# Second mixer and four norms of a two-block transformer kernel: one-column sums of squares, a factor spread by products with ones, and a new order of the second mixer's work

## The reference

```python
def rms_norm(x, gain=None):
    y = x * lax.rsqrt(jnp.mean(x * x, axis=-1, keepdims=True) + EPS)
    return y if gain is None else y * gain

def modulate(x, shift, scale):
    return rms_norm(x) * (1.0 + scale) + shift

# layer 0: mixer with latent attention and pooling, then ffn;  layer 1: gqa_mixer, then ffn
xl = xl + ml[:, 2] * mixer(modulate(xc, ..), modulate(xl, ml[:, 0], ml[:, 1]))
xl = xl + ml[:, 5] * conv_ffn(modulate(xl, ml[:, 3], ml[:, 4]), ..)
# (in layer 0 the context xc goes the same way)

def gqa_mixer(hc, hl, w_in, g_q, g_k, w_out, cos, sin):   # layer 1: 8 query heads, 2 key heads, width 128
    q = apply_rope(rms_norm(heads(hl @ w_in[:, :1024]), g_q), cos, sin)
    k = rms_norm(heads(h @ w_in[:, 1024:1280]), g_k)       # of context and of x; rotated for x alone
    v = heads(h @ w_in[:, 1280:])
    return softmax(q @ k.T / sqrt(128)) @ v @ w_out        # each query over 768 keys
```

## Time and profile before

| | before |
|---|---|
| median of three runs | 2988.4 us |
| profiled execution, its own time | 2990.08 us |
| its span in the profile | 2988.4 us |
| mean granted clock of TensorE, share of full speed | 0.956 |
| TensorE busy | 2739.5 us (92%) |
| VectorE busy | 1605.2 us (54%) |
| ScalarE busy | 1021.9 us (34%) |
| GpSimd busy | 81.9 us (3%) |

### The profile page before, as it was taken

One profiled execution on the slowest core, in us unless ns is written; L12 is line 12 of the kernel. 1 busy time (PEld: TensorE's weight loads), 2 busy tenths in 40 slices (PEclk: granted clock), 3 DMA queues, 4 the chain that ended last, 5 costly groups with the idle time before them and its releaser, 6 DMA issues. The chain is left out here.

```text
span 2988.4 us, 35774 instructions
## 1 busy us (share of the span) xinstructions
PE 2739.5 (92%) x14414; PEld 2206.9 (74%) x14414; DVE 1605.2 (54%) x2338; ACT 1021.9 (34%) x1595; POOL 81.9 (3%) x108
## 2 busy tenths in 40 slices
PE   5979988999999968887999998899988999999997
PEld 3758876888888857775788875688865777777775
DVE  5568745433433466765544444255545665565566
ACT  2135533222222233543323324422233433343343
POOL 0100000000000000000000000000000000000000
PEclk8979998999999979998999999999998999999998
DMA  5430012232332211001222223222221222222221
GB/s 209 142 113 29 20 45 99 100 119 99 113 116 103 89 39 43 29 34 38 88 96 92 92 85 113 77 85 85 88 91 49 87 77 74 80 87 80 85 74 43
DMA packets 67241, 246.94 MB, mean 83 GB/s; under 512 B 7504, under 2 KB 7888, under 8 KB 66384
## 3 DMA queue, kind: packets, MB, share of 16 engines
q1 hardware_dynamic: 51280, 185.10, 17.6%
q0 software_dynamic: 14768, 55.51, 5.9%
q10 hardware_dynamic: 1040, 4.12, 0.4%
HBM read 242.45 MB, written 2.24 MB: 82 GB/s over the span
## 5 line engine op out<-in xcount | busy, mean ns | idle before, releaser
L1966 DVE TENSOR_TENSOR WL<-RAW,WH 128x1024 fp32r<-128x1024 f32 x331 | 405.3, 1225 | 686.7 <-ACT WH L1417 685.1
L689 PE MATMUL PS<-HM,WH 128*128 128x512 f32 x1752 | 707.1, 404 | 23.3 <-DVE HM L1973 10.9
L690 PE MATMUL PS<-HM,WH 128*128 128x512 f32 x1752 | 699.5, 399 | 0.0
L691 PE MATMUL PS<-HM,WL 128*128 128x512 f32 x1752 | 698.7, 399 | 0.0
L1417 ACT ACTIVATE WH<-RAW 128x1024 fp32r<-128x1024 f32 x331 | 349.7, 1057 | 821.1 <-PE PS L691 810.4
L689 PEld LDWEIGHTS PS<-HM,WH 128*128 128x128 f32 x1752 | 333.5, 190 | 99.7 <-issue 34.2
L691 PEld LDWEIGHTS PS<-HM,WL 128*128 128x128 f32 x1752 | 333.1, 190 | 80.4
L690 PEld LDWEIGHTS PS<-HM,WH 128*128 128x128 f32 x1752 | 333.7, 190 | 56.0
L689 PE MATMUL PS<-GM,WH 128*128 128x512 f32 x468 | 189.1, 404 | 15.4 <-DVE X_M L2473 11.7
L691 PE MATMUL PS<-GM,WL 128*128 128x512 f32 x468 | 188.4, 403 | 0.0
L690 PE MATMUL PS<-GM,WH 128*128 128x512 f32 x468 | 188.4, 403 | 0.0
(11 more groups left out here) (366 smaller groups left out, 4621.0 us busy)
## 6 DMA issues: line engine op xcount, KB each, us to landing
RAW<-in_tiles SPq DMA_DIRECT2D x333, 512.0 KB, 3.2
MRAW<-in_mods POOLq DMA_DIRECT2D x80, 512.0 KB, 5.0
TB<-bias_rows POOLq DMA_DIRECT2D x16, 576.0 KB, 6.3
FIRST<-in_mods SPq DMA_DIRECT2D x8, 1024.0 KB, 23.8
X_M<-in_x ACTq DMA_DIRECT2D x1, 2048.0 KB, 16.7
VN_GB<-in_gm_rows POOLq DMA_DIRECT2D x2, 1024.0 KB, 6.0
out_x<-X_M SPq DMA_DIRECT2D x8, 256.0 KB, 2.0
X_C<-in_ctx ACTq DMA_DIRECT2D x1, 1024.0 KB, 19.8
```

Source lines behind the costliest of these rows:

```text
L689: pe.matmul(out_, wh, xh, start=first, stop=False, skip_group_check=True)
L690: pe.matmul(out_, wh, xl, start=False, stop=False, skip_group_check=True)
L691: return pe.matmul(out_, wl, xh, start=False, stop=last, skip_group_check=True)
L1966: dve.tensor_tensor(WL[:, s.mod(2), :], RAW[:, s.mod(2), :], f32(WH[:, s.mod(2), :]), ALU.subtract).then_inc(tile_split[s.mod(2)], 1)
```

## The change

**Norms (mix0, ffn0, mix1, ffn1).** VectorE leaves out the last of the seven adds: `SUMSQ` holds seven squares. TensorE's `norm_sum` multiplies each 128x128 block of `SUMSQ`, and of the last `SQ`, as stationary operand by one column of ones: 6 blocks (4 in ffn1) x 2, one column of PSUM per block, tokens on partitions. ScalarE's root and VectorE's inverse are of 128x6. VectorE multiplies the identity by that column, block by block (`RB`, 128x768, diagonal blocks; called the diagonal below), and TensorE's `norm_spread` multiplies ones by `RB`, so that every partition has the factor in PSUM, where `scaled` reads it. `add_square(m)` stands behind the next chunk's `add_gated`. In ffn0 `mod_rows(21)` stands between `norm_sum` and `norm_spread`.

**Key norms.** The same for each key head (`key_sums`, `key_scale`, `key_scales`); ScalarE copies the raw keys to SBUF, and `key_norm` scales that copy.

**Second mixer's start.** The value tiles and the first two query tiles change places in the list of tiles; queries 0 and 1 are made ahead of the values.

**Loop.** In pairs 0 to 2 each rotation is cut in two (`query_parts`, `query_turned`) and spread over units n = 2 to 7; before, both were whole at n = 2 and 4. In pair 3 the update of `X_M` (`part_added`) stands ahead of `pt_low`.

```diff
+            def norm_sum(name, ctx_too):
+                ...
+                    for b in range(low_block, BLOCKS):
+                        mm = pe.matmul(norm_sums(name)[:, b:b + 1], squares[:, b * P:(b + 1) * P], ONES[:, 0:1], start=first and b == low_block,
+                                       stop=last, skip_group_check=True)
+                ...
+                pe.wait_ge(sq_summed, (KC - 2) * (at + 1))
+                block_sums(SUMSQ, True, False)
+                pe.wait_ge(sum_sq, KC * (at + 1))
+                block_sums(SQ[:, (KC - 1) % 2, :], False, True).then_inc(sum_used, 1)
+
+            def norm_spread(name, ctx_too):
+                pe.wait_ge(diag_ready, SPREAD[name])
+                if ctx_too:
+                    pe.matmul(rb_ctx(name), ONES[:, :], RB[:, 0:TC], start=True, stop=True, skip_group_check=True)
+                pe.matmul(rb_main(name), ONES[:, :], RB[:, TC:TA], start=True, stop=True, skip_group_check=True).then_inc(rb_spread, 1)
...
-                stats(name, KC, ctx_too)
+                norm_sum(name, ctx_too)
                 if mods:
                     mod_rows(21)
+                norm_spread(name, ctx_too)
...
+                    if n == 1 and k == 2:
+                        key_sums(0)
+                    elif n == 1 and k == 6:
+                        key_scales(0)
...
-            key_sums(0)
-            tile_ready(s + 2)
-            tile_ready(s + 3)
-            v_step(0)
-            key_sums(1)
-            v_step(1)
-            v_step(2)
...
-            project(0)
+            project(0, 0, 9)
+            key_sums(1)
+            project(0, 9, 18)
+            key_scales(1)
+            project(0, 18, 24)
             project(1)
+            tile_ready(s + 4)
+            tile_ready(s + 5)
+            v_step(0)
             query_sums(0)
+            v_step(1)
+            v_step(2)
             scores(0)
...
                 dve.wait_ge(rms_ready, n + 1)
-                dve.reciprocal(RB[:, lo:TA], RB[:, lo:TA]).then_inc(rb_ready, 1)
+                root, blocks = NORM_ROOT[:, lo // P:BLOCKS], BLOCKS - lo // P
+                dve.reciprocal(root, root).then_inc(rb_ready, 1)
                 dve.wait_ge(rb_ready, n + 1)
+                dve.tensor_tensor(RB[:, lo:TA].rearrange("p (b n) -> p b n", b=blocks), IDENT[:, :].unsqueeze(1).to_broadcast([P, blocks, P]),
+                                  root.unsqueeze(2).to_broadcast([P, blocks, P]), ALU.mult).then_inc(diag_ready, 1)
...
-            def out_part(m):
+            def part_added(m):
...
+                if pair == 3 and n:
+                    part_added(n - 1)
                 pt_low(w)
                 if w >= 2 and w % 2 == 0:
                     out_low((w - 1) // 2)
                 if pair < 3:
                     if n == 2:
-                        split(At(TILES["gqa_q"] + j + 2))
-                        query_rope(j)
+                        query_parts(j)
                     elif n == 3:
+                        query_turned(j)
+                    elif n == 4:
+                        split(At(TILES["gqa_q"] + j + 2))
                         query_low(j)
-                    elif n == 4:
-                        split(At(TILES["gqa_q"] + j + 3))
-                        query_rope(j + 1)
                     elif n == 5:
                         scale_of_queries(pair + 1)
+                        query_parts(j + 1)
+                    elif n == 6:
+                        query_turned(j + 1)
+                    elif n == 7:
+                        split(At(TILES["gqa_q"] + j + 3))
                         query_low(j + 1)
...
-                    out_part(n - 1)
+                    next_out_tile(n - 1)
```

More of the change, by code:

```diff
@@ L429, in build, with query_tile @@
                 LOAD_ORDER[gmlp_out(g)[0].start + m] = TILES["gmlp"] + 12 * g + 8 + m
+        for n in range(2):
+            LOAD_ORDER[TILES["gqa_kv"] + 2 + n] = TILES["gqa_q"] + n
+            LOAD_ORDER[TILES["gqa_q"] + n] = TILES["gqa_kv"] + 2 + n
+        def query_tile(j):
+            return At(TILES["gqa_kv"] + 2 + j if j < 2 else TILES["gqa_q"] + j)
         assert sorted(LOAD_ORDER) == list(range(N_TILES))
@@ L535, in stat_ctx, with norm_sums, rb_main, rb_ctx @@
             return PS[:, 4 if name == "mix0" else 5, 0:TC]
+        BLOCKS, CTX_BLOCKS = TA // P, TC // P
+        def norm_sums(name):
+            at = TC if name == "mix0" else 0
+            return PS[:, 5 if name == "mix0" else 7, at:at + BLOCKS]
+        SPREAD = {name: n + 1 for n, name in enumerate(("mix0", "ffn0", "mix1", "key0", "key1", "ffn1"))}
+        NORM_ROOT = CONST[:, 11:11 + BLOCKS]
+        def rb_main(name):
+            return PS[:, 2, :] if name in SUMMED else RB[:, TC:TA]
+        def rb_ctx(name):
+            return PS[:, 5, 0:TC] if name in SUMMED else RB[:, 0:TC]
         MOD_SUMS = PS[:, 6, 0:2 * P]
@@ L801, in _ @@
                 first_rows(pair)
+                if pair == 7:
+                    norm_spread("mix0", True)
                 first_turn(pair - 1)
@@ L804, in _ @@
                     pe.wait_ge(bias_ready, 1)
[L805 removed]
+                    norm_sum("mix0", True)
             first_turn(7)
@@ L1044, in key_sums, with key_scales @@
                     pe.wait_ge(head_rms, n)
[L1045 to L1046 removed]
+                for b in range(BLOCKS):
+                    mm = pe.matmul(key_cols(n)[:, b:b + 1], SQ[:, n, b * P:(b + 1) * P], ONES[:, 0:1], start=True, stop=True, skip_group_check=True)
+                mm.then_inc(head_sum, 1)
+            def key_scales(n):
+                pe.wait_ge(diag_ready, SPREAD[f"key{n}"])
+                pe.matmul(PS[:, 5, 0:TC], ONES[:, :], RB[:, 0:TC], start=True, stop=True, skip_group_check=True)
+                pe.matmul(PS[:, 4, :], ONES[:, :], RB[:, TC:TA], start=True, stop=True, skip_group_check=True).then_inc(rb_spread, 1)
             s = At(TILES["gqa_kv"])
@@ L1457, in root @@
                     act.wait_ge(sum_used, SUMMED.index(name) + 1)
-                else:
-                    act.wait_ge(sq_used, c0 + chunks)
+                    blocks = slice(0 if ctx_too else CTX_BLOCKS, BLOCKS)
+                    act.activation(NORM_ROOT[:, blocks], norm_sums(name)[:, blocks], ACT.Sqrt, bias=CONST[:, eps:eps + 1], scale=1.0 / features
+                                   ).then_inc(rms_ready, 1)
+                    return
+                act.wait_ge(sq_used, c0 + chunks)
                 if SPLITS.get(name, 0):
@@ L1747, in next_out_tile, with key_high @@
                     kept_chunks(m + 2)
-            v_taken(0)
-            v_taken(1)
-            for n in range(2):
+            def key_high(n):
                 act.wait_ge(rope_done, 10 + n)
@@ L1754, in _ @@
                 copy(KG[0][:, n, TC:TA], RG[0][:, :]).then_inc(key_hi, 1)
-                if n == 0:
-                    v_taken(2)
-                    for j in range(2):
-                        split(At(TILES["gqa_q"] + j))
+            key_high(0)
             query_taken(0)
+            key_high(1)
+            query_taken(1)
+            v_taken(0)
             query_high(0)
-            query_taken(1)
             root_of_queries(0)
             query_high(1)
+            v_taken(1)
+            v_taken(2)
+            for j in range(2):
+                split(At(TILES["gqa_q"] + 2 + j))
             exps(0)
@@ L2374, in down @@
                         add_gated(u + m, layer, 5, At(m), ctx_too)
+                        if before is not None and m:
+                            add_square(before, m - 1, 0 if ctx_too else TC)
                         if ahead and (m + 1) % per_tile == 0:
                             split(s + m // per_tile + 2)
-                        if before is not None:
-                            add_square(before, m, 0 if ctx_too else TC)
                 for f in range(FC):
@@ L2409, in _ @@
             s = At(TILES["gqa_kv"])
-            for n in range(2):
-                split(s + 2 + n)
             dve.wait_ge(norm_ready, SPLITS["ffn1"])
@@ L2478, in out_part @@
                     kept_chunks(m + 2)
+            split(s + 2)
+            key_scale(0)
             key_norm(0)
-            v_read(0)
+            split(s + 3)
+            key_rope(0)
+            key_scale(1)
             key_norm(1)
-            v_read(1)
-            key_rope(0)
-            v_read(2)
-            for j in range(2):
-                split(At(TILES["gqa_q"] + j))
+            split(s + 4)
             key_rope(1)
@@ L2494, in _ @@
             dve.tensor_scalar(ROPE_TG[:, 1, :], ROPE_TG[:, 1, :], LN[:, 2, 16:17], None, ALU.mult).then_inc(rope_gain, 1)
-            query_rope(0)
+            split(s + 5)
+            query_parts(0)
+            query_turned(0)
             query_low(0)
-            split(At(TILES["gqa_q"] + 2))
-            query_rope(1)
+            query_parts(1)
+            query_turned(1)
+            v_read(0)
             scale_of_queries(0)
             query_low(1)
```

(5 more changed lines are left out.)

108 lines of the change are left out of this document (68 added, 40 removed).

## The result

Four runs of the changed kernel: median 2950.03 us (2948.74 to 2953.86), beside 2990.18 for four of the kernel before; ratio 0.9868, 95% interval 0.9851 to 0.9885. A second set of four (e10) gave 2951.8 and 0.9874 (0.9858 to 0.9891). The prediction was 2959.3, within 2943 to 2975: the direction and this range held. The profiled execution has a span of 2952.2 us, 36.2 less than before's.

What follows compares the result with a forecast made beforehand. TensorE, busy for 2739.5 of 2988.4 us, was taken as the bound. Seven terms summed to -29.1 us, giving 2959.3 against the median of 2988.4; own range 2951 to 2966, widened by rivals to 2943 to 2975.

Steps and rivals of the forecast that it cites:

- seven terms: Forecast by stretch: mix1 -5.4, mix0 -1.1, ffn0 -1.5, ffn1 -6.0, start +6.5, loop -5.8, pair 3 -15.8 us.
- One sign of being right: In the changed profile, the loop's longest wait for `PTA` would be near 1 us.
- term of the output with ffn1: Output's updates and ffn1's norm: later adds and a smaller inverse give -6.0 us (-6.6 to -4.2).
- mix0: Norm of mix0: scaled chunks start 1.1 us earlier, -1.1 (-3.6 to +1).
- mix1: Norm of mix1: compact inverse and later adds against 24 one-column instructions, -5.4 us (-7.6 to -2).
- ffn0: Norm of ffn0: spread waits behind the second module rows' transfer, chunks begin 1.5 us sooner, -1.5 (-3 to 0).
- Start: Second mixer's start: old waits go, two new stalls from VectorE's order come, +6.5 us (-5 to +8).
- Rival 1: Second mixer's start pays, no stalls: -5 us there and not +6.5, 2948 in all; chance 0.14.
- Loop: Pairs 0 to 2: wait for `PTA` falls from 4.8 to about 1.1, -5.8 us (-14.5 to 0).
- Pair 3: Pair 3: TensorE's waits for `X_M` and the low clock behind them go, -15.8 us (-8 if `pt_low` takes half).
- Rivals 2, 3 and 4: 2: loop and pair 3 return less, 2973, chance 0.16; 3: clock stays low, slower, 0.03; 4: norms return nothing, 2971, 0.07.

Runs made afterwards that it cites:

- e10: The changed kernel run again, unedited: median 2951.8 us, ratio 0.9874 to the kernel before.
- e3: The kernel before with only the four norms changed: median 2969.15 us, ratio 0.9931.
- e5: The changed kernel with the second key's inverse and diagonal put ahead of the first key's low parts on VectorE: median 2946.38 us, ratio 0.9866.
- e6: The changed kernel with the second mixer's start reordered at both places where TensorE waited: median 2942.81 us, ratio 0.985.
- e2: The kernel before with only the loop's query rotations cut in two and spread over units 2 to 7: median 2979.89 us, ratio 0.9968.
- e4: The kernel before with only the second mixer's start changed: median 2991.9 us, ratio 1.001.
- e1: The kernel before with only pair 3's residual update put ahead of the transposed rows' low part: median 2973.63 us, ratio 0.9939.
- e7: The changed kernel with six products of each pair's second query moved from unit 2 to unit 3 in the loop: median 2951.2 us, ratio 0.9869.
- e11: The kernel before, unedited, once more for one profile: pair 3 took 72.4 us, where the first profile had 73.9.
- e8: The changed kernel with the edits of e6 and e7, and ffn0's spread ahead of the second module rows: median 2941.66 us, ratio 0.9843.

## Why the prediction was right, and what it mis-sized

**The places.** All seven terms have the right sign, and the waits named came where they were put: 4.1 and 3.7 us in the start (4.3 and 3.9 forecast), none for `X_M` over 0.3 in pair 3. One sign of being right failed: the loop's longest wait for `PTA` is 3.1 us and not near 1. The errors don't cancel: five terms were too small a gain or too large a loss by 1 to 3.5 us each, and only pair 3's was too large a gain, by 0.6 to 2.1.

**Norms.** The term of the output with ffn1 held (6.0, measured 6.0). mix0 can be read once the thirteen profiles are sorted by how long TensorE is busy before its sums: 21.2 us in five, 26.6 in eight, and both norms occur in both groups. Where it is 26.6, the first product behind the norm comes at 63.5 to 64.2 us in the five profiles with the old norm and at 61.1 to 61.7 in the three with the new one. Where it is 21.2, it comes at 59.2 in the one profile with the old norm, and with the new one at 56.2, 56.4, 56.8 and, in e3, at 59.2. So mix0 gave about 2.5 us where 1.1 were forecast, with one profile that shows none of it; some 1.5 lies ahead of the sums and so outside the table's stretch. mix1 gave 6.7 and not 5.4: the sums came 0.7 us earlier than I had them, and their first half ran faster, 12 instructions in 1.74 us and only the other 12 in 2.70. I had priced all 24 at 0.21 us, 5.1 in all; they end 4.3 after their start. The low-clock price itself is nearly right (0.225 an instruction for my 0.21; the bounds were 0.115 and 0.23). The Trainium skill's figure for a load of 128 columns that names no clock ("TensorE: Matmul & The Clock Gate", "LDWEIGHTS (loading the stationary operand)") does not hold at the lower clock: 12 loads would take 1.3 us by it, an estimate from its 107 ns, and the second twelve of mix1's norm took 2.68 at PEclk 0.50. ffn0 gave 2.5 and not 1.5: I had held the second module rows to the transfer's landing, 6.9 us behind its issue (468.5 to 475.4); in the changed kernel it landed after 5.9 (465.5 to 471.5), and the spread came that microsecond sooner.

**Start.** +6.5 was +5.1, and 0.8 less again from `scores(0)` to the first transposes. The waits and the clock behind them were nearly right (1.5 us on the spread, where I had 1.7, and 1.3 on the first value step, where I had 1.5); the order was the cause (e5, e6). The terms of that step add up to 6.1 and its chain of times to 6.4, not 6.5. Measured against its terms, idle time rose by 1.4 us (1.8 forecast) and TensorE's busy time by 3.7 (4.3 forecast). Rival 1, the start without its stalls, is what e6 is: 3.1 us less than before, where I had given 5.

**Loop.** This is the step that failed in size: 5.8 forecast, 9.3 measured, whole by itself (e2). The step counted waits, and waits fell by 6.2 us, near the forecast: idle time was 21.6 before (131.07 less 109.47 busy) and is 15.4 after (121.80 less 106.40). What it left out stood in the earlier trace rows: transposes that took 1.51 us behind the wait of 4.8, at the lower clock, for 0.84 now. TensorE's busy time fell by 3.1 us with the same instructions, and that is clock. I had added that price in the start and in pair 3 and not here. In the old loop slower products do cost time, because behind the long wait TensorE sets the pace: units 6 and 7 of pair 0 take 10.5 us there with 0.3 of idle time, and the old loop of e4, busy for 0.8 us less with the same idle time, is 0.8 shorter. In the new loop they no longer do: these units take 10.9 us with 2.4 of idle time, and the whole loop of e6, at clock 1.00, is as long as the changed kernel's at 0.98.

```profile
1164.84:1286.62 121.78, 105.16 (x669) 90.36 (x668) 91.23 (x171) 69.95 (x115) 0.00 (x0) 1.00 0.07 22
```

**Pair 3.** 15.8 forecast; 15.2 less than the first profile of before and 13.7 less than the second, 16.6 and 15.0 in e1. The old order takes 71.1 to 73.9 us in six profiles, with 12.6 us of idle time in each: up to 2.8 us of it is what the clock happened to be. I had taken the low clock of the longest of them (5.82 and 7.07 us) as a fixed price. And the new loop takes 1.3 us back in the first unit of pair 3, which is 9.65 for 8.31 in e1. That is VectorE's order and not the clock: in e7, with the clock at 1.00 all through pair 3, the unit takes 9.66 too, with a wait of 1.31 for `GM`.

**Sum.** The stretches with an edit give -36.4, where the terms gave -29.1: loop 3.5, start 2.1, mix1 1.3, ffn0 1.0, pair 3 -0.6. The second pair of profiles (e11 and e10) gives -34.6. What the timed runs show beyond that, 2 to 6 us, is in part mix0's earlier sums (some 1.5) and otherwise within what the stretches without an edit differ by from one execution to the next. Rivals 2, 3 and 4 did not come: the mean clock went from 0.956 to 0.967 and 0.969.

## What to carry to other kernels

When a wait on TensorE goes, count the slower products behind it too, in every stretch alike, but only where TensorE sets the pace: where it waits again soon after, the lower clock uses up that wait and costs nothing (e7 and e8, pair 0). So don't read idle time turned into busy time as a loss before a second profile, at another clock, has shown the stretch to be longer. In a hand-ordered queue look for a small instruction that another engine waits for behind a long group that nobody waits for yet: the second key's inverse behind a rotation, the residual update behind `pt_low`, each add behind its own square; in the norms moving it was worth as much as the new arithmetic. Compare two kernels by stretches between the same events, with a second profile of each: unedited stretches differed here by 2 to 5 us between two profiles of one kernel, and by 7 over all thirteen. Sorting many profiles by what happened ahead of a stretch can show a gain that two can't (mix0).

## What the runs showed of the hardware

- One-column fp32 products with a 128x128 stationary operand: 12 instructions in 1.39 us at full clock, 2.70 at PEclk 0.50. Their twelve weight loads take 2.68 us there.
- The granted clock falls without a long idle stretch ahead: in e7 it is 0.71 in the mean from 1204 to 1209 us, behind waits of 0.8 and 1.0 us, and 0.50 from 1241 to 1246, around a wait of 0.8, where the changed kernel keeps 1.00 around waits of the same length in its first two pairs. What decides it was not tried and stays open. The Trainium skill ("TensorE: Matmul & The Clock Gate", "HAM oscillation — how this bites in real kernels") names long idle stretches as the cause of such falls; e7's falls have none ahead of them.
- A lower clock can leave the time as it is: pair 0 takes 38.03 us at 0.96 with 2.3 of idle time (e7) and 38.04 at 1.00 with 3.7 (e8), in the same code.
- In the first 45 us the products of the module rows took 1.04 us for 16 in one profile of the kernel before and 1.89 in the other, though the window from 24 to 41 us has PEclk 0.80 in the first and 1.00 in the second: there the recorded clock does not go with the speed. The one-column sums of mix0 stand there too: 24 instructions take 5.25 us in the changed kernel, with PEclk 1.00 in the record, and 5.25 in e3, with PEclk 0.50.
